# Moving the four tiles of split weights to other byte offsets in SBUF

## What is computed

```python
proj = xn @ w_in[l]                                   # and w_out, xa_w_q, xa_w_kv, xa_w_o
g    = fn @ ffn_w_gate[l]
h    = h + (silu(g_conv) * (fn @ ffn_w_up[l])) @ ffn_w_down[l]
proj = hn @ w_in                                      # even and odd layer, and both w_out
```

## Time and profile before

| | |
|---|---|
| median of 3 runs (lowest to highest) | 3233.27 us (3232.43 to 3237.83) |
| the profiled execution, its own time | 3238.98 us |
| its span, first to last instruction | 3237.2 us |
| mean granted TensorE clock | 0.969 of full speed |
| TensorE matmul busy | 3041.2 us, 94% |
| VectorE, ScalarE, GpSimd busy | 58%, 29%, 25% |
| DMA | 53 GB/s in the mean |

### The profile page before, as it was taken

One profiled execution on the slowest core, in us unless ns is written; L12 is line 12 of the kernel. 1 busy time (PEld: TensorE's weight loads), 2 busy tenths in 40 slices (PEclk: granted clock), 3 DMA queues, 4 the chain that ended last, 5 costly groups with the idle time before them and its releaser, 6 DMA issues. The chain is left out here.

```text
span 3237.2 us, 38700 instructions
## 1 busy us (share of the span) xinstructions
PE 3041.2 (94%) x15406; PEld 2448.9 (76%) x15406; DVE 1875.2 (58%) x2775; ACT 951.9 (29%) x1837; POOL 808.5 (25%) x478
## 2 busy tenths in 40 slices
PE   7999998988999999999899999998998999999888
PEld 6777787767788888888677777776676777777667
DVE  4334565543754154254588888887444367777774
ACT  3232344324211000011333333333222344444431
POOL 3121000141433333323233333332233211111101
PEclk9998999989999999999999999998999999999899
DMA  3002000010211111112211211122332100000021
GB/s 125 33 33 95 14 1 14 20 59 27 72 45 52 46 52 46 53 51 78 72 46 45 73 47 71 45 73 98 111 98 72 42 31 27 27 28 32 7 79 65
DMA packets 47738, 170.26 MB, mean 53 GB/s; under 512 B 5200, under 2 KB 5472, under 8 KB 46688
## 3 DMA queue, kind: packets, MB, share of 16 engines
q1 hardware_dynamic: 45856, 161.85, 14.2%
q0 software_dynamic: 1728, 6.29, 0.5%
HBM read 145.06 MB, written 23.07 MB: 52 GB/s over the span
## 5 line engine op out<-in xcount | busy, mean ns | idle before, releaser
L194 PE MATMUL acc<-x_hi,w_hi 128*128 128x512 f32 x2048 | 833.0, 407 | 53.8 <-POOL w_lo L189 23.1
L187 POOL CAST w_hi<-w_raw 128x1024 fp32r<-128x1024 f32 x217 | 239.9, 1106 | 2356.2 <-PE acc L196 1397.2
L195 PE MATMUL acc<-x_lo,w_hi 128*128 128x512 f32 x2048 | 808.9, 395 | 0.0
L196 PE MATMUL acc<-x_hi,w_lo 128*128 128x512 f32 x2048 | 808.6, 395 | 0.0
L189 POOL TENSOR_TENSOR w_lo<-w_raw,w_hi 128x1024 fp32r<-128x1024 f32 x217 | 544.2, 2508 | 17.4
L194 PEld LDWEIGHTS acc<-x_hi,w_hi 128*128 128x128 f32 x2048 | 391.5, 191 | 150.9 <-issue 42.3
L196 PEld LDWEIGHTS acc<-x_hi,w_lo 128*128 128x128 f32 x2048 | 391.1, 191 | 84.4
L195 PEld LDWEIGHTS acc<-x_lo,w_hi 128*128 128x128 f32 x2048 | 392.1, 191 | 79.5 <-issue 2.4
L2513 DVE SCALAR_TENSOR_TENSOR acc<-ev_upad,cols,acc 128x1024 f32<-128x1024 f32 x232 | 298.3, 1286 | 5.0
L194 PE MATMUL aux<-x_hi,w_hi 128*128 128x512 f32 x464 | 198.1, 427 | 2.3 <-POOL w_lo L189 2.3
L196 PE MATMUL aux<-x_hi,w_lo 128*128 128x512 f32 x464 | 184.2, 397 | 0.0
(11 more groups left out here) (506 smaller groups left out, 4998.6 us busy)
## 6 DMA issues: line engine op xcount, KB each, us to landing
w_raw<-in_stream SPq DMA_DIRECT2D x217, 512.0 KB, 3.4
h<-in_x SPq DMA_DIRECT2D x16, 512.0 KB, 9.7
spill_h<-h SPq DMA_DIRECT2D x8, 512.0 KB, 5.4
spill<-ev_zst SPq DMA_DIRECT2D x8, 512.0 KB, 3.1
h_even<-spill_h SPq DMA_DIRECT2D x8, 512.0 KB, 8.1
ev_zr<-spill SPq DMA_DIRECT2D x8, 512.0 KB, 3.4
spill_h<-h_even SPq DMA_DIRECT2D x8, 512.0 KB, 5.4
h<-spill_h SPq DMA_DIRECT2D x8, 512.0 KB, 4.3
```

What stands on the lines that cost most here:

```text
L187: pool.tensor_copy(k.w_hi[slot][:], k.w_raw[slot][:]).then_inc(k.w_split, 1)
L194: pe.matmul(out, w_hi, x_hi, start=start, stop=False)
L195: pe.matmul(out, w_hi, x_lo, start=False, stop=False)
L196: return pe.matmul(out, w_lo, x_hi, start=False, stop=stop)
```

## The change

The four weight tiles are placed by hand in one ring in which each has 128 bytes more than it needs. Tile number n of the ring (`w_hi[0]`, `w_hi[1]`, `w_lo[0]`, `w_lo[1]`) begins `W_SHIFT[n]` words of 4 bytes after n x 4224 bytes. As 4224 is a multiple of 128, the starts modulo 128 are 8, 0, 4 and 24 words: 32, 0, 16 and 96 bytes. (The change was announced as 32, 0, 0 and 96; the third tile is allocated at offset 0, and its slice begins four words further.) The ring makes everything behind it 512 bytes longer, and the arena is now rounded up to a multiple of 256 bytes. By the sizes in the code it moves by 512 bytes in relation to `h`. Instructions, their order, their shapes and their waits stay.

```diff
 ROW_BYTES = 4 * HALF
+W_PAD = 32
+W_SHIFT = (8, 0, 4, 24)
...
-        pool.tensor_copy(k.w_hi[slot][:], k.w_raw[slot][:]).then_inc(k.w_split, 1)
+        pool.tensor_copy(k.w_hi[slot], k.w_raw[slot][:]).then_inc(k.w_split, 1)
         pool.wait_ge(k.w_split, n * 2 + 1)
-        pool.tensor_tensor(k.w_lo[slot][:], k.w_raw[slot][:], k.w_hi[slot][:].bitcast(F32),
+        pool.tensor_tensor(k.w_lo[slot], k.w_raw[slot][:], k.w_hi[slot].bitcast(F32),
                            ALU.subtract).then_inc(k.w_split, 1)
...
-        k.w_hi = [sbuf(f"w_hi{i}", [P, KD * P], F32R) for i in (0, 1)]
-        k.w_lo = [sbuf(f"w_lo{i}", [P, KD * P], F32R) for i in (0, 1)]
+        ring_at = nc.sbuf_base
+        sbuf("w_ring", [P, 4 * (KD * P + W_PAD)])
+
+        def ring_tile(name, n):
+
+            first = W_SHIFT[n] % 8
+            at = ring_at + 4 * (n * (KD * P + W_PAD) + W_SHIFT[n] - first)
+            return nc.alloc_sbuf_tensor_at(name, [P, KD * P + 8], F32R, offset=at)[:, first:first + KD * P]
+        k.w_hi = [ring_tile(f"w_hi{i}", i) for i in (0, 1)]
+        k.w_lo = [ring_tile(f"w_lo{i}", 2 + i) for i in (0, 1)]
...
-        arena = -(-nc.sbuf_base // ROW_BYTES) * ROW_BYTES
+        arena = -(-nc.sbuf_base // (2 * P)) * (2 * P)
```

## The result

The changed kernel takes 3272.82 us (median of 4 runs, 3252.71 to 3280.05) against 3232.85 us for the kernel before (median of 4): a ratio of 1.0117, 95% interval 1.0078 to 1.0155. (The ratios here are estimated from the single runs and differ a little from the quotient of the medians, which is 1.0124.) The forecast was 3204.3 with a range up to 3260; the time is that of the slower rival, 3272. The profiled execution took 3277.73 us, its span is 3276.0, 38.8 us longer than before.

The account below looks back on a forecast made before the run. The prediction took TensorE's matmul step, 226.7 ns, to bound the kernel. Savings of 9.4 us in the feed-forward and 19.6 us outside, together 29.0, took the median 3233.27 to 3204.3 us; range 3160 to 3260, the forecast's own 3165 to 3223.

Parts of the forecast that it names:

- the slower rival: Changed offsets keep matmul chains unsettled at 231 ns, 4.3 ns more each: 39 us, 3272 us; chance 0.23 in either form.
- What bounds the kernel: TensorE, busy 94% of the span: time is close to the number of matmuls times their step, 226.7 ns settled.
- The reading of the surplus: In each matmul step, 13.3 ns are no streaming: weight load and moving stream wait for each other, in 6.67 ns rounds.
- one round off in one slot and two in the other: Product triples lose 10 ns each in the mean, step 223.3 ns: 9.4 us in the feed-forward, 19.6 us outside.
- The lower bound: For the product step: a plain float32 matmul leaves 3.0 ns of surplus, so some 10 of 13.3 ns can go.
- If only the position modulo 128 counts: Condition under which moving arena and constants by 512 bytes changes nothing for VectorE, ScalarE and the DMAs: 0 taken.
- The arena: Arena and constants moving by 512 bytes in relation to `h`: 0 taken, no more than 3 us either way.
- The split on GpSimd: Weight split writing at new offsets, 1106 + 2508 ns per tile: no change taken; 10% longer would cost 3 us.
- its milder form: Product triples take one round more, 2.2 ns per matmul: 20 us, 3253 us; shares the 0.23 for slower.
- It decides from the point where the settled mean step is above 226.7: Sign in the matmul chains: a settled mean step above 226.7 ns means the slower outcome, chance 0.23.
- No effect: Matmul surplus is the price of exchanging weights, or depends on time: step stays 226.7 ns, 3233 us; chance 0.14.
- Much faster: Reads in the matmuls no longer meet, surplus falls to 3.0 ns: 90 us less, 3144 us; chance 0.13.

Follow-up runs that it names:

- the scans: Kernels of nothing but product triples, output a copy of the input, with operand offsets varied (127 settings, chosen byte offsets, 240 random settings): lowest step 226.7 ns.
- e_zero: The changed kernel with all four weight offsets at 0, padding and arena move kept: 3249.21 us, ratio 1.005 to the kernel before.

## Why the prediction was wrong

*What bounds the kernel* was right: TensorE's step times the number of matmuls. 42.0 us more on TensorE made the span 38.8 us longer. If the 14.6 us of the feed-forward all went through, outside it 24.2 of 27.4 did, 88%, between the 85% of the forecast and the 90% of the slower rival.

*The reading of the surplus* was half right. The step depends on where the operands start, and the time goes in rounds of 6.67 ns. That the 13.3 ns of the settled step are themselves a meeting of reads, no run shows, since no placement brought any of them back. Most steps of the scans are whole numbers of rounds over a triple or two (226.7, 228.9, 231.1, 233.3 are 102, 103, 104 and 105 rounds per triple).

*The failed step is the one that took "one round off in one slot and two in the other".* That the slots would lock to whole rounds, and differently, came true; the direction didn't. The slots gained 13.6 and 17.2 ns per triple (231.2 and 232.4 against 226.7), two rounds and some two and a half more, where -6.67 and -13.33 were taken. The argument was that a lost meeting should be worth at least one round. But equal offsets were not a collision that could be lost: at multiples of 32 bytes they gave the shortest pattern of over 400 settings. No row of the trace of before showed an unequal one, and the only rows with longer steps, 231 ns after a wait, were put to the rival. The lower bound was also less near than it looked. The 16 plain float32 matmuls of the earlier trace rows make 32 records, whose starts lie 429 ns apart, so a record there is half a matmul. 429 less two passes of 213.3 (the prediction's estimate) leaves 2.4 ns per weight load, where the prediction had 3.0, but for another kind of matmul; no run gave float32r any of that gain.

*"If only the position modulo 128 counts"* was the second fault, and the offsets were worked out modulo 128 throughout. The period is 256 bytes, so that the ring's padding of 128 bytes per tile does harm by itself: 0.5% in e_zero with every offset at 0. The forecast put nothing on the padding, and slot 1 of the change had its tiles at 128 and 224, not at 0 and 96.

*The arena* was right: 512 bytes are two periods, 1.0012 (0.9999 to 1.0026). *The split on GpSimd* too: 2518 against 2508 ns, 26.0 against 25.1 us of waits.

*The rivals.* The slower one came true in its direction and nearly in its price: 4.3 ns per matmul by its working, 5.2 measured in the feed-forward and 4.1 outside, 3272 against 3272.82 us. That the totals agree so closely is luck: the 4.3 ns were the mean of ten steps after one wait, too little inside the feed-forward and a little too much outside. Its mechanism, a chain thrown out again by each triple, is not what the trace shows, since both slots repeat a pattern; nearer is its milder form, whole rounds more per triple, with two or more where it took one. "It decides from the point where the settled mean step is above 226.7" was the right place to look. That a change of offset within the triple does it is also too narrow: equal offsets of both weight tiles cost as well (233.3 at 32 bytes), since the distance to the activations counts. That rival had 0.23. "No effect" is out: moving nothing but the weights' start by 128 bytes makes the step 5.7 ns longer. The Trainium skill says that a weight load takes nothing from the running matmul ("TensorE: Matmul & The Clock Gate", "What happens when you issue a matmul"). What the prediction drew from it, that offsets change nothing, is contradicted here. Whether the weight load and the running matmul are what gets in each other's way is not shown: moving the low activations alone does the same (233.3 ns). "Much faster" is out for every placement tried.

## What to carry to other kernels

When a chain of equal instructions runs at one exact step, look at what it does just after a disturbance: if the steps there are longer, the steady state is a locked one. A change that breaks the symmetry of the operands can then cost such longer steps for good, as it did here, and needs a reason of its own to be counted as a gain. For products in float32r (the reduced float32 format) with 512 columns, place weights and activations at equal offsets modulo 256 bytes and at multiples of 32, padding included, and check any new ring or pool of tiles for its pitch. Beyond that no placement tried here gains: 226.7 ns was the lowest settled step in over 400 settings.

## What the runs showed of the hardware

As long as the starts are multiples of 128 bytes, only their differences modulo 256 count: 128 bytes on the weights (232.3 to 233.3 ns), on the activations (232.3 to 232.4) or on either low part alone (231.1 and 233.3) all spoil the step, 128 on all four doesn't. A common start of 16 or 48 bytes does spoil it (230.0 to 233.3).

The chain seems to rest against something that runs by itself. Take the starts of the 9936 product matmuls before the change modulo a cycle of 6.67 ns (its length fitted to within two millionths): 63% lie in one eighth of the cycle. Stage by stage, across the waits between them, the share in that same eighth is 50 to 84%, except in the attention of the odd layer (2560 to 3040), where it is 22%. The starts of the other matmuls are spread over all eighths (9 to 16% each). In the changed kernel the fullest eighth holds 23%. What the cycle is, and why it goes with 256 bytes and not with 128, no run here tells.

The changed kernel's four runs spread over 27 us. More than half of that goes with the granted clock again: 3252.71 us at 0.976, 3267.92 at 0.972, 3280.05 and 3277.73 at 0.968 and 0.967, where the kernel before has some 16 us between 0.975 and 0.968. Whether an execution can also fall into another pattern stays open, as only one of them has a trace.
